# Layer 0's later modulation vectors move from TensorE's projection stage to GpSimd beside the MLP, and the projection's first two weight tiles are multiplied in the opening

## What is computed

```
mx = jnp.split(cond_x @ ada_w[i] + ada_b[i], 6, axis=-1)
mc = jnp.split(cond_c @ ada_w[i] + ada_b[i], 6, axis=-1)
hx = modulate(rms_norm(x, g[0]), mx[0], mx[1])
hc = modulate(rms_norm(ctx, g[0]), mc[0], mc[1])
...
x = x + mx[2] * rms_norm(ox, g[1])
x = x + mx[5] * rms_norm(sq_relu_mlp(modulate(rms_norm(x, g[2]), mx[3], mx[4]), ff_w1[i], ff_w2[i]), g[3])
```

## Time and profile before

| | |
|---|---|
| median of three runs | 3459.39 us (3456.45 to 3461.07) |
| profiled execution: span on the core, its only time on the page | 3457.7 us |
| TensorE busy | 3317.7 us, 96% of the span |
| VectorE / ScalarE / GpSimd busy | 53% / 37% / 20% |
| moved by DMA | 406.6 MB, mean 118 GB/s |

### The profile page before, as it was taken

The page is one execution under the profiler, slowest core; times in us unless marked ns, Lnnn a source line. Parts: engine busy times, 40 slices in busy tenths (PEclk is TensorE's granted clock), DMA queues, the critical chain, the costliest instruction groups (busy, mean ns, idle before and its releaser), DMA issues. The chain is left out here.

```text
span 3457.7 us, 39533 instructions
## 1 busy us (share of the span) xinstructions
PE 3317.7 (96%) x15472; PEld 2443.2 (71%) x15472; DVE 1818.6 (53%) x2304; ACT 1291.3 (37%) x2118; POOL 691.5 (20%) x383
## 2 busy tenths in 40 slices
PE   6999999999999999999999999898999999999998
PEld 3666444555788888888889878652456788888886
DVE  3233544433555544554586444588576654445444
ACT  4333344445553333333454223452113532233332
POOL 0000478667331101300120100110011320002001
PEclk8999999999999999999999999999999999999999
DMA  8753533321253333433465311102513333333333
GB/s 329 290 214 103 179 65 77 77 61 48 98 171 127 112 97 97 146 98 96 131 195 175 113 62 39 51 1 101 203 49 109 132 126 97 98 98 117 121 98 104
DMA packets 134552, 406.62 MB, mean 118 GB/s; under 512 B 24153, under 2 KB 38265, under 8 KB 130016
## 3 DMA queue, kind: packets, MB, share of 16 engines
q1 hardware_dynamic: 134368, 404.11, 36.1%
HBM read 345.05 MB, written 58.92 MB: 117 GB/s over the span
## 5 line engine op out<-in xcount | busy, mean ns | idle before, releaser
L1598 PE MATMUL psum<-hid_high,w_high_and_low 128*128 128x512 f32 (+1 forms) x1536 | 416.3, 356 | 11.7 <-DVE hid_low L1831 9.4
L1581 PE MATMUL psum<-h_high,w_high_and_low 128*128 128x512 f32 (+1 forms) x1536 | 415.6, 356 | 0.7 <-DVE w_high_and_low L1741 0.7
L1648 ACT ACTIVATE w_high_and_low<-w_raw 128x1024 fp32r<-128x1024 f32 x226 | 238.6, 1056 | 342.3 <-PE psum L1598 238.8
L1853 POOL TENSOR_TENSOR squares_then_rstd_of_out<-squares_then_rstd_of_out,square_out 128x512 f32<-128x512 f32 (+1 forms) x69 | 103.2, 1495 | 1277.1 <-ACT square_out L1663 1277.1
L1741 DVE TENSOR_TENSOR w_high_and_low<-w_raw,w_high_and_low 128x1024 fp32r<-128x1024 f32 x226 | 285.7, 1265 | 90.9 <-ACT w_high_and_low L1648 90.2
L1313 POOL TENSOR_TENSOR probs_added<-probs_added,probs_turned 128x1024 f32<-128x1024 f32 x128 | 308.1, 2407 | 66.6 <-ACT probs_turned L1238 54.0
L1598 PEld LDWEIGHTS psum<-hid_high,w_high_and_low 128*128 128x128 f32 x1536 | 274.2, 190 | 54.5 <-DVE hid_low L1831 7.8
L1581 PEld LDWEIGHTS psum<-h_high,w_high_and_low 128*128 128x128 f32 x1536 | 273.1, 189 | 42.5 <-DVE w_high_and_low L1741 1.3
L1280 DVE TENSOR_REDUCE row_max<-psum 128x1 f32<-128x1280 f32 x120 | 179.0, 1492 | 228.5 <-PE psum L1176 137.2
L1828 DVE TENSOR_TENSOR hid_high<-hid_relu_and_square 128x512 fp32r<-128x512 f32 (+1 forms) x160 | 111.5, 697 | 351.3 <-ACT hid_relu_and_square L1731 351.2
L1598 PE MATMUL psum<-hid_low,w_high_and_low 128*128 128x512 f32 (+1 forms) x768 | 272.2, 354 | 0.0
(11 more groups left out here) (472 smaller groups left out, 6713.0 us busy)
## 6 DMA issues: line engine op xcount, KB each, us to landing
w_raw<-in_ff_w_dram SPq DMA_DIRECT2D x320, 512.0 KB, 3.6
ada_ring<-in_ada_w_dram SPq DMA_DIRECT2D x24, 2048.0 KB, 9.8
w_raw<-in_w_out_dram SPq DMA_DIRECT2D x38, 512.0 KB, 3.5
scratch_spectra<-spectrum_out SPq DMA_DIRECT2D x32, 256.0 KB, 2.0
filter_ring<-scratch_spectra SPq DMA_DIRECT2D x16, 512.0 KB, 3.9
stream_in<-scratch_x SPq DMA_DIRECT2D x27, 256.0 KB, 4.4
w_raw<-in_w_hy_dram SPq DMA_DIRECT2D x12, 512.0 KB, 3.9
scratch_hyena<-mixed SPq DMA_DIRECT2D x12, 512.0 KB, 2.6
```

The lines of the kernel that those rows point to most:

```text
L1581: mm = pe.matmul(bank[:, 0:n], x[i % SLOTS][:, k, :], y[:, k, a:a + n], start=(k == 0 and m == 0), stop=(k == KT - 1 and m == 2))
L1598: mm = pe.matmul(bank[:, 0:n], x[i % SLOTS][:, 2 * k + half, :], y[:, k, 0:n], start=(k == 0 and m == 0), stop=(k == HT - 1 and m == 2))
L1648: act.activation(w_hi[i % SLOTS], raw[i % 2], ACT.Copy).then_inc(w_rounded, 1)
L1853: pool.tensor_tensor(acc_out[:, q % 2, 0:n], acc_out[:, q % 2, 0:n], sq_out[:, v % 2, 0:n], ALU.add).then_inc(added_out, 1)
```

## The change

- `ADA_FIRST` keeps eight pieces and `ADA_LATER` two. The other twelve, (0, 10 and 11) and all of layer 1, are made in layer 0's `out_and_mlp` by GpSimd, in 112 granules of 256 KB (one feature tile of one piece). For each stream a granule takes a `tensor_scalar` (weights times the conditioning value of the partition) and, but for the first granule of a piece, a `tensor_tensor` add to an accumulator, each 128 x 512. 48 granules serve two streams (four operations, three steps in four), 64 serve one (two operations, one a step). They stand at steps 2-4, 6-8, 14-16, 18-20, 22-24, 35, 37, 39-41, 43-45, 56-58 and on to 98, 108 to 151, 160-162 and 179 to 195; the steps of `norm_beside` have none. Five batches (at steps 36, 67, 97, 139, 196) end in four matmuls that add over the partitions, a ScalarE copy, four that turn, and one to four small VectorE operations.
- SP loads each granule at its step, behind that step's weight tile, and waits first for GpSimd to be done with the granule two before.
- The opening loads, rounds and splits the first two weight tiles and multiplies both with chunk 0 (`first_unit`). ScalarE's and VectorE's orders there change, and `project_attention` starts at unit 2 for TensorE.
- A DMA scratch area is made smaller, which frees SBUF.

```
-ADA_FIRST = [(0, piece) for piece in (2, 3, 0, 1, 4, 5, 6, 7, 8, 9)]
-ADA_LATER = [(0, piece) for piece in (10, 11)] + [(1, piece) for piece in range(ADA_PIECES)]
+ADA_FIRST = [(0, piece) for piece in (2, 3, 0, 1, 4, 5, 6, 7)]
+ADA_LATER = [(0, piece) for piece in (8, 9)]
+END_OF_ADA = 212
+ADA_BESIDE = [(0, (10, 11), (0, 1)), (1, (2, 3), (0, 1)), (1, (0, 1), (0, 1)), (1, (4, 5, 6, 7), (0,)), (1, (8, 9, 10, 11), (0,))]
...
+                def first_unit(t):
+                    a, n = spans[0]
+                    pe.wait_ge(w_split, t + 1)
+                    pe.wait_ge(split, KT)
+                    pe.wait_ge(logged, t + 1)
...
-                for i in range(NEEDED, A):
+                ada.multiply(pe, 4)
+                ada.turn(pe, 4)
+                add_squares(2, range(0, 4))
+                first_unit(0)
+                ada.multiply(pe, 5)
+                add_squares(2, range(4, KT))
+                first_unit(1)
+                ada.turn(pe, 5)
+                for i in (6, 7):
                     ada.multiply(pe, i)
+                for i in (6, 7):
                     ada.turn(pe, i)
...
                 root(1)
-                shift(0, range(4, KT))
-                of_x(2)
-                shift(1, range(0, 4))
+                ada.copy(act, 4)
+                act.wait_ge(w_first, 32)
+                for t_first in range(2):
+                    act.activation(g.first_high[:, t_first], g.first_raw[:, t_first], ACT.Copy).then_inc(w_rounded, 1)
+                for k in range(KT):
+                    of_x(2, (k,))
+                    shift(1, (k,))
                 root(2)
...
+    units = [(0, *c0), (1, *c0), (0, *c1), (0, *c2), (1, *c1), (1, *c2)] + [(t, a, n) for t in range(2, TILES) for a, n in CHUNKS]
...
+    norm_beside = [(KT + 1, KT + 5), (26, 35), (46, 55), (88, 96), (99, 108), (152, 160), (163, 179), (212, END_OF_ADA)]
...
+                def load_granule(m):
+                    b, of_layer, piece, k = granules[m]
+                    if m >= 2:
+                        sp.wait_ge(mod_stepped, ops_by[m - 2])
+                    sp.dma_start(mod_raw[:, m % 2, :], ada_w[of_layer * ADA_PIECES + piece][:, k, :]).then_inc(mod_in[m % 2], 16)
...
+                def add_over_rows(i):
+                    bank = bank_for(unit_of[i, "mod"])
+                    pe.wait_ge(mod_stepped, batch_ops[mod_at[i]])
+                    for x in range(4):
+                        mm = pe.matmul(bank[32 * x:32 * x + 32, :], g.ones[:, 0:32], mod_acc[:, x, :], start=True, stop=True, tile_position=(0, 32 * x))
+                    mm.then_inc(product, 1)
+
+                def turn_rows(i):
+                    bank = g.ps[:, unit_of[i, "mod"] % BANKS, :]
+                    pe.wait_ge(mod_copied, mod_at[i] + 1)
+                    for m in range(4):
+                        mm = pe.matmul(bank[:, 4 * m:4 * m + 4], mod_row[:, m * P:(m + 1) * P], g.ident[:, 0:P:32], start=True, stop=True)
+                    mm.then_inc(mod_turned, 1)
...
+                def add_granule(m):
...
+                    for s in streams:
+                        total = mod_acc[:, MODS[b][1].index(piece) * len(streams) + s, :]
+                        scaled_w = total if k == 0 else w if s == streams[-1] else mod_row[:]
+                        if n:
+                            pool.wait_ge(mod_stepped, n)
+                        pool.tensor_scalar(scaled_w, w, g.cond[:, k, s:s + 1], None, ALU.mult).then_inc(mod_stepped, 1)
+                        n += 1
+                        if k:
+                            pool.wait_ge(mod_stepped, n)
+                            pool.tensor_tensor(total, total, scaled_w, ALU.add).then_inc(mod_stepped, 1)
+                            n += 1
```

More of the change, by code:

```diff
@@ L235, in _, with add_squares @@
             def _(pe):
-                def add_squares(c):
+                def add_squares(c, tiles=range(KT)):
                     a, n = spans[c]
-                    for k in range(KT):
+                    for k in tiles:
                         q = c * KT + k
@@ L1332, in out_and_mlp @@
     N = len(steps)
-    units = [(i, half) for i, (c, e, j) in enumerate(steps) for half in range(1 if e is None or (c is not None and j < HT) else 2)]
+    MODS = ADA_BESIDE if ada_w is not None else []
+    norm_beside = [(KT + 1, KT + 5), (26, 35), (46, 55), (88, 96), (99, 108), (152, 160), (163, 179), (212, END_OF_ADA)]
+    quiet = [i for i in range(2, END_OF_ADA) if not any(a <= i < b for a, b in norm_beside)]
+    granules, mod_at, granule_at = [], {}, {}
+    at = 0
+    for b, (of_layer, of_pieces, streams) in enumerate(MODS):
+        for piece in of_pieces:
+            for k in range(KT):
+                if len(streams) > 1 and at % 4 == 3:
+                    at += 1
+                granule_at[quiet[at]] = len(granules)
+                granules.append((b, of_layer, piece, k))
+                at += 1
+        mod_at[quiet[at]] = b
+        at += 1
+    ops_of = [len(MODS[b][2]) * (1 if k == 0 else 2) for b, of_layer, piece, k in granules]
+    ops_by = [sum(ops_of[:m + 1]) for m in range(len(granules))]
+    batch_ops = [max(ops_by[m] for m in range(len(granules)) if granules[m][0] == b) for b in range(len(MODS))]
+    units = []
+    for i, (c, e, j) in enumerate(steps):
+        units += [(i, half) for half in range(1 if e is None or (c is not None and j < HT) else 2)]
+        if i in mod_at:
+            units.append((i, "mod"))
     unit_of = {x: u for u, x in enumerate(units)}
@@ L1339, in kind @@
         return "next" if c is None else "out" if e is None else "up" if j < HT else "down"
-    released = {"out": 0, "up": 0, "down": 0, "next": 0}
+    released = {"out": 0, "up": 0, "down": 0, "next": 0, "mod": 0}
     release = []
     for i, half in units:
-        released[kind(i)] += 1
-        release.append((kind(i), released[kind(i)]))
+        what = "mod" if half == "mod" else kind(i)
+        released[what] += 1
+        release.append((what, released[what]))
     def at_step(c, e, j):
```

130 lines of the change are left out of this document (97 added, 33 removed).

## The result

The changed kernel takes 3477.07 us, the median of four runs (3474.41 to 3480.38), against 3457.92 (3455.77 to 3461.07) for the kernel before on the same chip: ratio 1.0057, 95% interval 1.0043 to 1.0071. The forecast was 3448.4 us with a range that ended at 3469, so both its sign and its range were wrong.

The account below looks back on a forecast made before the run. TensorE, busy 96% of the span, was taken as the bound. The terms -33.5 + 9.5 + 1 + 4 + 8 = -11.0 us, off the median 3459.4, gave 3448.4 us, with a range of 3431 to 3469 for 8 in 10 runs.

Parts of the forecast that it names:

- What bounds the kernel: Whole span: TensorE busy 96%, GpSimd 20%; the projection bound by TensorE, the opening a chain of loads, ScalarE and VectorE.
- The front: Opening, seam and projection together: twelve pieces leave (-37.8), +2, +4 and -1.7, in all -33.5 us.
- The norm chain: Projection: swaps wait for their norm in shortened steps, +2 us (0 to 9); rival with waits of 9, 3454 us, chance 0.15.
- The opening: Stage before the projection: two pieces fewer, two products more, ending near 83 us against 79.2, +4 us (-2 to +8).
- The slow matmuls: Seam into the projection: after TensorE's wait a dozen matmuls start 0.43 us apart, not 0.23, costing about 2.4 us.
- The batches: MLP: five batches of adding over rows and turning on TensorE, 1.9 us each, +9.5 us.
- the scaling's price: GpSimd's 128 x 512 scaling in the granules: between 0.43 and 1.30 us, taken as 0.85, so a two-stream granule takes 4.3.
- the context's output steps: Steps 14 to 28: ScalarE's squares wait for GpSimd's adds and weight loads have little slack, +4 us (0 to 16).
- the wide steps: Wide MLP steps: TensorE's 18 matmuls of cover mostly absorb VectorE's hold-ups, +1 us over some 14 groups (0 to 4).
- The narrow MLP steps: Steps 160-162 and 179-195: GpSimd's granules hold VectorE up some 0.4 us a step, +8 us (2 to 16).
- GpSimd sets the pace: Rival for the output steps and MLP: granules of 7 to 8 us make others wait, 3470 us, slower; chance 0.24.
- Whether a one-input operation holds VectorE up: Granules in the output steps and MLP: left open whether GpSimd's scaling delays VectorE as its add does; no row showed it.

Follow-up runs that it names:

- `e_short_early`: The changed kernel with GpSimd's granules at steps 2 to 25, all but the first of each piece, cut to 64 of 512 columns: 3450.74 us, ratio 0.9987.
- `e_short_narrow`: The changed kernel with GpSimd's granules from step 152 on, all but the first of each piece, cut to 64 of 512 columns: 3465.22 us, ratio 1.0023.

## Why the prediction was wrong

**What bounds the kernel** was read rightly: the front lost what its TensorE work was worth, and the loss sits in the stage that receives it.

**The front, forecast -33.5, measured -43.6** in the changed kernel's trace. The pieces were 3.24 us each where 3.15 was taken (-38.9 in place of -37.8). The norm chain cost nothing where +2 was taken: the swap without modulation ahead waited 1.13 us at the end of the stage, as in the earlier trace rows, and the key product came 38.9 earlier. The opening ended at 82.2 where 83 was expected, and unit 2 began at 105.66 against 105.61 before: together they cost 0 and not +2.3. The slow matmuls that were charged behind the wait did come (the two pieces took 3.29 and 3.05 us in place of 1.92); shorter was the way there. The first piece's load was issued 4.1 us behind the opening's end (82.2 to 86.27), not 5.1 as before (79.2 to 84.27), and the second piece waited 0.43 us for a bias and not for its load. This zero is one execution's: unit 2 begins anywhere from 101.6 to 108.1 us in the same code. Another 4.7 us were in no term: 1.0 in the next stage's first wait (2.69 in place of 3.69, and 2.69 to 2.72 in all thirteen profiles without the twelve pieces), and 3.7 behind it. Of these, 2.4 are that stage's first twelve starts, 0.23 us apart (199.38 and on) where they had been 0.43 apart (239.51, 239.94). The 3.7 are no effect of the change that can be told from chance: from that stage's first product to the first add of squares the kernel before took 650.2 us and the changed one 646.5, and the twelve experiments 645.9 to 650.5, in the same code.

**The batches, forecast 1.9 each, measured 2.2** by two stretches of two batches each.

**The step that failed is the scaling's price.** "It is over 0.43 (one column) and at most the add's 1.30; I take 0.85": the upper end was argued, since an add reads twice as much, and no row showed it. The operation takes 1.56 alone and 2.0 in place. The estimate from the GPSIMD Engine Reference of the Trainium skill (Performance versus the Vector engine), 0.6 us, was further off still. With 0.85 the granule was 4.3 us and not the measured 6.8, and two terms fell: the context's output steps, forecast +4, measured +27.3 (26.3 by `e_short_early`); and the wide steps, forecast +1, measured 10.8 + 4.5 less four batches of 2.2, some +6.5. The narrow MLP steps, forecast +8 with a range of 2 to 16, were 15.9 less one batch, some +14 (11.9 by `e_short_narrow`), inside its range. The row of 15.9 is good to some 5 us only.

**The rival "GpSimd sets the pace" described what happened**, down to its condition ("once a scaling takes near 1.3 us"), to granules of 7 to 8 us (5.9 to 8.9 in GpSimd's timeline from 937 to 973 us), to ScalarE's squares behind GpSimd in steps 20 to 27, and to its place. It had 0.24 because the condition was judged by the guessed price. Its size was short too: 16 us in that place, where 27 came, because it had counted ScalarE's squares and the first residual add, and not SP, whose weight loads queue behind its wait for GpSimd's granule, and not the clock, 8.1 of the 27.3. Its 3470 us came near the truth by luck: it had the costs 14 us too small (44.5 for 58.5) and the front's gain 10 too small.

**Whether a one-input operation holds VectorE up**, left open in the prediction, is answered: hardly (1239 against 1223 ns for a split in the mean), while the two-input add does, as the earlier trace rows had shown. The one-input operation is lengthened by VectorE, though, from 1.56 to 1.9 or 2.1.

## What to carry to other kernels

When the price of an operation that is in no row decides between two cases, do not close its range with an argument: let the range go past the nearest row, and give the rival that lives there its share. An engine at a third of its time over the whole span can be full in the few steps that matter, so lay its queue out by stretch, with everything that waits for it, the loads' issuing engine too. And before moving work to an idle engine, ask whether the busier one does it in a single instruction: 0.75 us on VectorE stood against 3.4 on GpSimd.

## What the runs showed of the hardware

- GpSimd's `tensor_scalar` of 128 x 512 float32 with one value a partition took 1.56 us alone, more than its `tensor_tensor` of the same size (1.26). VectorE's took 0.48.
- VectorE and GpSimd disturb each other by kind: GpSimd's adds lengthened VectorE's two-input operations (746 to 870 ns for `h_low`), its scalings hardly did (752), and both of them were lengthened themselves (adds to 1.64, scalings to 1.88 and 2.08 in the mean, in the runs with one of them alone).
- Waiting TensorE lost again afterwards: with 20.2 us idle in 173.6 the granted clock was 0.94, and the same 722 matmuls were busy 153.4 us in place of 145.3.
- The same code varied from one execution to the next in the opening: the granted clock of its first 40 us was 0.95 in one profile and 0.87 in another, and the same matmul behind it started at 101.6 us in the one and at 108.1 in the other.
